# A mixture-of-experts kernel: the slot list of an expert is made at another place, and the gather skips empty slots

## The reference

```python
aff = softmax(tok @ router_w)                        # 512 x 16
best = argmax(sum of the two best experts, per group of 4)
idx  = the two best experts inside group best        # top-2
w    = aff[idx] / sum(aff[idx])
for e in range(16):
    gate, up = split(tok @ w_gu[e], 2)               # 1024 -> 2 x 512
    out += comb[:, e] * ((silu(gate) * up) @ w_down[e])   # 512 -> 1024
x = layer_norm(ALPHA * x + g2 * out)
```

## Time and profile before

| | us |
|---|---|
| median of 3 runs | 1605.09 (1601.73 to 1605.34) |
| the profiled execution, device time | 1602.93 |
| its span, first to last instruction | 1601.2 |
| MoE of layer 0, first row transposes to last matmul | 349.95 to about 666 |
| MoE of layer 1, first row transposes to the result rows | 1230.51 to about 1545 |

### The profile page before, as it was taken

One profiled execution on the slowest core, in us unless ns is written; L12 is line 12 of the kernel. 1 busy time (PEld: TensorE's weight loads), 2 busy tenths in 40 slices (PEclk: granted clock), 3 DMA queues, 4 the chain that ended last, 5 costly groups with the idle time before them and its releaser, 6 DMA issues.

```text
span 1601.2 us, 17947 instructions
## 1 busy us (share of the span) xinstructions
PE 1253.5 (78%) x6409; PEld 973.3 (61%) x6409; DVE 1101.4 (69%) x1201; ACT 770.8 (48%) x964; POOL 267.0 (17%) x330
## 2 busy tenths in 40 slices
PE   0499969249999999519966899999914999999950
PEld 0377748127777777317964676776812777777730
DVE  5558674738888898583645676654473888888837
ACT  0223322217777777432422455566221777777732
POOL 2011110300000000130000454544030000000012
PEclk8599989569999999759957799999956999999975
DMA  8567853309999999832311232322430999999942
GB/s 299 201 220 235 276 189 145 117 29 344 377 389 393 384 389 397 298 130 77 116 49 38 83 105 94 105 106 80 145 118 29 351 391 382 393 389 388 393 166 84
DMA packets 107406, 355.99 MB, mean 222 GB/s; under 512 B 7746, under 2 KB 16062, under 8 KB 107342
## 3 DMA queue, kind: packets, MB, share of 16 engines
q1 hardware_dynamic: 82920, 268.47, 44.7%
q0 software_dynamic: 19568, 69.78, 12.6%
q10 hardware_dynamic: 4854, 16.88, 2.6%
HBM read 329.89 MB, written 25.21 MB: 222 GB/s over the span
## 4 chain that ended last, share of the span: by engine, by line
PE 43%; issue 21%; DVE 18%; DMA 7%; ACT 7%; POOL 3%; ACTq 1%; DVEq 0%; POOLq 0%; SPq 0%
PE bank L203 11%; PE bank L205 10%; PE bank L204 10%; DVE acc L318 3%; PE bank L1713 2%; ACT w_hi L939 2%; PE bank L1731 2%; DMA xg<-scratch_u,tok 2%; DVE xt L432 1%; DMA raw<-in_w_down_dram 1%; DVE ln_stat L404 1%; PE bank L1701 1%; DMA ada<-in_ada_w_dram 1%; DVE us L386 1%; POOL prob L1945 1%
## 5 line engine op out<-in xcount | busy, mean ns | idle before, releaser
L945 DVE TENSOR_TENSOR w_lo<-raw,w_hi 128x2048 fp32r<-128x2048 f32 x189 | 433.5, 2298 | 83.6 <-ACT w_hi L939 83.6
L939 ACT ACTIVATE w_hi<-raw 128x2048 fp32r<-128x2048 f32 x189 | 362.3, 1918 | 86.8 <-PE bank L205 76.5
L203 PE MATMUL bank<-w_lo,xe_hi 128*128 128x512 f32 x512 | 212.0, 414 | 5.8 <-DVE xe_lo L902 5.3
L205 PE MATMUL bank<-w_hi,xe_hi 128*128 128x512 f32 x512 | 203.9, 398 | 0.0
L204 PE MATMUL bank<-w_hi,xe_lo 128*128 128x512 f32 x512 | 203.7, 398 | 0.0
L198 DVE TENSOR_TENSOR w_lo<-raw,w_hi 128x2048 fp32r<-128x2048 f32 x37 | 85.3, 2310 | 153.4 <-ACT w_hi L193 153.0
L193 ACT ACTIVATE w_hi<-raw 128x2048 fp32r<-128x2048 f32 x37 | 70.4, 1909 | 160.6 <-PE bank L205 158.9
L203 PE MATMUL bank<-u_lo,w_hi 128*128 128x512 f32 x320 | 133.4, 417 | 12.7 <-DVE q L1615 9.3
L875 POOL DMA_INDIRECT xg<-scratch_u,tok x32 | 33.9, 1058 | 602.5 <-DVE tok L869 601.9
L205 PE MATMUL bank<-u_hi,w_hi 128*128 128x512 f32 x320 | 129.8, 406 | 0.0
L204 PE MATMUL bank<-u_hi,w_lo 128*128 128x512 f32 x320 | 129.8, 406 | 0.0
(11 more groups left out here) (255 smaller groups left out, 2345.0 us busy)
## 6 DMA issues: line engine op xcount, KB each, us to landing
raw<-in_w_gu_dram SPq DMA_DIRECT2D x128, 1024.0 KB, 8.1
raw<-in_w_down_dram SPq DMA_DIRECT2D x64, 1024.0 KB, 8.4
ada<-in_ada_w_dram POOLq DMA_DIRECT2D x64, 512.0 KB, 5.7
scratch_y<-ye ACTq DMA_DIRECT2D x32, 512.0 KB, 7.6
ada<-in_ada_w_dram SPq DMA_DIRECT2D x32, 512.0 KB, 3.8
raw<-in_conv_w_in_dram SPq DMA_DIRECT2D x12, 1024.0 KB, 10.2
rows<-scratch_mods POOLq DMA_DIRECT2D x12, 512.0 KB, 4.6
raw<-in_w_kv_dram SPq DMA_DIRECT2D x6, 1024.0 KB, 8.6
```

The costliest lines, as they stand in the source:

```text
L203: nc.tensor.matmul(o, lh, rl, start=start, stop=False)
L205: return nc.tensor.matmul(o, lh, rh, start=False, stop=stop)
L939: nc.scalar.activation(w_hi[:, hslot, :], raw[:, slot, :], ACT.Copy).then_inc(hi_done, 1)
L945: nc.vector.tensor_tensor(w_lo[:, slot, :], raw[:, slot, :], w_hi[:, hslot, :].bitcast(F32), ALU.subtract).then_inc(lo_done, 1)
```

## The change

The matrix `oneh` of expert e+3 is now made where expert e's list used to be read (after `ht_lo`); the list matmuls of e+2 are PE's first instructions in expert e; and DVE reads the list as its first instruction in expert e. The row transposes of e+1, which write bank 7, therefore wait for the list of e+2 instead of that of e+1. `posm` gets a 17th row of -1, for the one-hot matrix of an expert that isn't there. The second token column starts at -4096 and `list_dve` adds 4096, so that an empty slot comes out as 4096 instead of 0, and the gather is bounded: indices over 511 are left out.

```diff
-        posm = rnew("posm", [P, NE, TT])
+        posm = rnew("posm", [P, NE + 1, TT])
...
-            it(tokc[:, :, 1:2], [[P, TT], [0, 1]], 0, 0).then_inc(s.consts.sem, 1)
+            it(tokc[:, :, 1:2], [[P, TT], [0, 1]], -NOTOK, 0).then_inc(s.consts.sem, 1)
...
+            go(V.memset(posm[:, NE, :], -1.0))
...
-            nc.vector.tensor_scalar(tok[:, p, :], bank[7][:, 0:1], bank[7][:, 1:2], None, ALU.add)
+            nc.vector.tensor_scalar(tok[:, p, :], bank[7][:, 0:1], bank[7][:, 1:2], float(NOTOK), ALU.add, ALU.add)
...
-                                    in_offset=bass.IndirectOffsetOnAxis(ap=tok[:, p, :], axis=0)
+                                    in_offset=bass.IndirectOffsetOnAxis(ap=tok[:, p, :], axis=0),
+                                    bounds_check=SEQ - 1, oob_is_err=False
...
-        def rows_pe(pe, s, pair, p):
+        def rows_pe(pe, s, pair, p, next_listed):
...
-            pe.wait_ge(*s.tok_made.at(2 * pair + p + 1))
+            pe.wait_ge(*s.tok_made.at(2 * pair + p + 1 + next_listed))
...
         def expert_pe(pe, s, pair, p, last=False):
             e, q = 2 * pair + p, 1 - p
+            more = not (isinstance(pair, int) and pair == PAIRS - 1)
+            if more:
+                list_pe(pe, s, pair + 1, p)
             gate_up(pe, s, pair, p, 0, p, 2)
             if not last:
-                rows_pe(pe, s, pair + p, q)
+                rows_pe(pe, s, pair + p, q, more)
             gate_up(pe, s, pair, p, 1, p, 3)
             if not last:
                 pe.wait_ge(*s.xe_lo_made.at(e + 2))
                 after(pe, s.h_made, e)
                 gate_up(pe, s, pair, p, 2, q, 0)
-            if not (isinstance(pair, int) and pair == PAIRS - 1):
-                list_pe(pe, s, pair + 1, p)
...
         def expert_dve(dve, s, pair, p, last=False):
             e = 2 * pair + p
             if not (isinstance(pair, int) and pair == PAIRS - 1):
-                one_hot(dve, s, pair + 1, p)
+                list_dve(dve, s, pair + 1, p)
...
             if not (isinstance(pair, int) and pair == PAIRS - 1):
-                list_dve(dve, s, pair + 1, p)
+                one_hot(dve, s, pair + 1 + p, 1 - p)
             for i in range(5, 9) if not last else range(4, 7):
                 step_lo(dve, s, pair, p, i)
...
             list_dve(dve, s, 0, 1)
+            one_hot(dve, s, 1, 0)
             rows_dve(dve, s, 0, 0)
```

More of the change, by code:

```diff
@@ L42 @@
 LIMIT = CAP
+NOTOK = 4096
 EBLK = 6
@@ L103, in __init__ @@
             def __init__(self, name, total=0):
+                self.name = name
                 if name not in Count.pool:
@@ L111, in at, with more @@
                 return self.sem, self.base + value
+            def more(self, n):
+                Count.pool[self.name][1] += n
         w_lo_at = place[0]
@@ L710, in __init__ @@
                  self.sg_made, self.h_made, self.h_turned, self.ht_hi_made, self.ht_lo_made, self.y_made) = each.values()
+                self.oh_made.more(1)
                 self.y_w1, self.res = Count("moe_y_w1", TT), Count("moe_res", TT)
@@ L868, in list_dve @@
             after(dve, s.xg_in[p], 16 * pair)
-            nc.vector.tensor_scalar(tok[:, p, :], bank[7][:, 0:1], bank[7][:, 1:2], None, ALU.add).then_inc(s.tok_made.sem, 1)
+            nc.vector.tensor_scalar(tok[:, p, :], bank[7][:, 0:1], bank[7][:, 1:2], float(NOTOK), ALU.add, ALU.add).then_inc(s.tok_made.sem, 1)
         def gather(pool, s, pair, p):
@@ L1291, in moe_pe @@
             pe.wait_ge(*s.tok_made.at(2))
-            rows_pe(pe, s, 0, 0)
+            rows_pe(pe, s, 0, 0, True)
             begin_pe(pe, s)
```

## The result

| | before | changed |
|---|---|---|
| median, us | 1604.16 (4 runs) | 1652.68 (4 runs, 1651.14 to 1652.84) |
| span of the profiled execution, us | 1601.2 | 1649.4 |

The ratio is 1.0304, 95% interval 1.029 to 1.0318: 3% slower. Forecast were 1651 us, range 1636 to 1668.

What follows compares the result with a forecast made beforehand. PE was taken to bound the MoE loops. Terms 48.9 - 1.6 - 0.5 + 0.4 = +47.2 us on the profiled 1602.93 us made 1650.1, put at 1651 us as median; range 1636 to 1668.

Steps and rivals of the forecast that it cites:

- Who sets the pace: In the two MoE loops PE, not the weight transfers, sets an expert's period, 18.9 us before the change.
- B: Rival: transfers set the loops' period, so skipped rows save 0.64 us per expert, -20 us, 1582 us; chance 0.05.
- The wait for the list: Row transposes wait for DVE's list reading, some 1.8 us in each of 28 periods, 48.9 us in all.
- Rival C: PE makes good part of the wait, 0.43 us back per period, -12 us, 1638 us; chance 0.08.
- The four matmuls: List matmuls at the expert's head: 0 as the wait covers them, 0.43 us without that wait.
- The one-hot matrix behind `ht_lo`: On DVE, 0.48 us more ahead of the next remainder, which PE needs only later: cost 0.
- The gather: Issued some 8 us earlier in the loop, bounded at 0.94 to 2.74 us on POOL, covered by slack: 0.
- The first gather: Each layer's exposed first gather: skipped half shortens it, -0.5 us for both layers, between 0 and -1.3.
- The extra one-hot matrix: In the prologue, 0.69 us on DVE, run while the first gather is under way: 0.
- Ends of the layers and prologue: Earlier last gather relieves late loads, -1.6 us; shorter first gathers, -0.5; memset in the router's chain, +0.4.
- The clock: PE's clock stays at 1.00 in the loops despite idling some 1.4 us in each period.
- A: Rival: PE's clock falls in the new gap, 1.5 us more per period, +43 us, 1694 us; chance 0.10.

Runs made afterwards that it cites:

- e9: Kernel before with the bounded gather; one-hot matrix, list matmuls and list reading keep their old places but serve e+3 instead of e+2: 1599.21 us, ratio 0.9971.
- e10: Kernel before, one-hot matrix, list matmuls and list reading at their old places but one expert further ahead, without bound and 4096: 1602.11 us, ratio 0.9994.
- e2: Changed kernel with the new order alone, without the bound and 4096, so 128 rows in each gather: 1653.29 us, ratio 1.0313 to the kernel before.
- e4: Changed kernel, but the list of e+2 goes to a free gate bank instead of bank 7, so row transposes don't wait for it: 1605.14 us, ratio 1.0006.
- e3: Changed kernel, but DVE reads the list one instruction earlier, ahead of the previous expert's last weight remainder; bank 7 stays: 1606.66 us, ratio 1.0007.
- e8: Changed kernel with three extra copies on DVE ahead of the list's reading, making the row transposes' wait longer: 1666.05 us, ratio 1.0391 to the kernel before.
- e5: Kernel before with four extra small matmuls, results unused, at the head of experts 0 to 13: 1609.79 us, ratio 1.0041.
- e1: Kernel before with the bounded gather alone (empty slots 4096, left out), order of PE and DVE untouched: 1621.63 us, ratio 1.0117.
- e6: Kernel before with the bounded gather, but DVE reads the list ahead of `ht_lo` instead of behind it: 1600.85 us, ratio 0.9985.

## Why the prediction was right, point by point

- **Who sets the pace.** PE, not the transfers: right. e9 and e10 differ by 8.4 MB of transfers and not at all in mid loop; B's 20 us aren't there.
- **The wait for the list.** Sized at 48.9 us. From the first to the last row transposes the layers grew by 24.65 us (280.55 to 305.20) and 25.34 us (279.14 to 304.48), together 50.0 us. e2 shows it whole without the other part of the change, e4 and e3 show it gone when either link is cut, e8 that it is passed on in full. The sum was 1.1 us short: I let PE follow the list by 0.06 us, which it did in 12 periods, while in 16 it took 0.14 or 0.15, some 1.4 us in all. Rival C, 0.43 us given back per period, didn't occur: the path from row to `hh` transposes stayed at 6.97 to 7.19 us in 27 of the 28 periods (7.38 in one), where before it was 6.94 to 7.36. The four matmuls would cost up to 0.19 us without the wait (e4, e5), not the 0.43 us of the prediction.
- **The one-hot matrix behind `ht_lo`.** 0, right: in the period shown the remainder follows it at once, and from 385 to 631 us PE never waits for `w_lo`.
- **The gather.** 0 for the loop of the changed kernel, right (e2 against the changed kernel). The reason that I gave was thin: I took the 2.74 us of the slowest gather as a bound and didn't ask what had made it slow. It was the same hold-up: that gather starts at 375.88, 0.36 us into a remainder that starts at 375.52. In e1 it cost 16 us. In the changed kernel no gather of the loop meets it, and it would have had more than 10 us of slack.
- **The first gather**, -0.5 us for skipped rows: wrong. It still takes 4.2 us and more to land (4.24 and 4.46 us in the two layers, 4.16 and 4.21 before), and from the reading of the list to the landing it is 0.2 and 0.3 us longer. POOL's queue has 19568 packets as before, only the bytes fell, 69.78 to 61.40 MB. The extra one-hot matrix, which I put at 0, stands in its way:

```profile
345.31 0.68 DVE L861 TENSOR_TENSOR oneh<-slots,posm 128x512 bf16<-128x512 f32 x1
```

```profile
345.70 1.24 POOL L882 DMA_INDIRECT xg<-scratch_u,tok  x1 [41.69 <-DVE tok L876]
```

The gather starts 0.39 us into it and ends 0.95 us behind it; before, it took 1.02 us.
- **Ends of the layers and prologue.** Forecast -1.6 - 0.5 + 0.4 = -1.7 us; the span's growth of 48.2 less 50.0 is -1.8. That the total fits is in part luck. From the last row transposes to the last down matmul the layers are 1.1 and 1.3 us shorter, together 2.4 instead of 1.6; everything else around the loops is 0.6 us longer instead of 0.1 shorter.
- **The clock.** No fall at waits of 1.48 to 1.63 us, right; e8 shows that 0.3 us more starts it in some periods. A was nearer than its chance of 0.10 suggests.

## What to carry to other kernels

In a software pipeline that is full, the price of a new wait is the distance between two instructions in one period of the old trace: where the awaited result would stand in its engine's order, less where the waiting one starts now. It costs its whole length each time if the awaited engine is itself tied to the waiting one. To start something earlier, move it by a whole period at its old place rather than within the period to a place where others queue for the same bank or engine. That keeps the loss away; what it gains is another matter, here 0.3% with the skipped rows (e9) and nothing without them (e10).

## What the runs showed of the hardware that I had not expected

- A bound on the indirect gather delays its start on POOL from 0.27 to 0.76 us after the index is written, and adds 0.05 us to its own time (0.94 to 0.99 us).
- A bounded gather that starts 0.5 us into a 2.29 us DVE instruction with two SBUF inputs takes 2.64 us and ends 0.86 us behind it (e1); one that starts 0.08 us ahead takes 0.99 us (e6), and an unbounded one 0.01 us behind its start 0.94 us (the kernel before).
- Rows left out by the bound save bytes, not packets: as many packets as before, 2049 more of them under 512 bytes.
- PE waits of 1.5 to 1.6 us in periods of 20.6 us left the clock at 2.4 GHz in all 28 periods; waits of 1.8 to 1.9 us (e8) brought it to 1.2 GHz in 5 of 28.
